# MoBA's attention scores in fp32r, from high and low parts of queries and keys with three products each, instead of fp32

## The reference, cut to what matters

```python
q_g, k_g, v_g, g_g, gk_lr, q_m, k_m, v_m = jnp.split(xn @ w_in, split_points, axis=-1)
scale = hd ** -0.5
s_own = (jnp.einsum('bhqd,bhsd->bhqs', qi, k_own, preferred_element_type=jnp.float32) * scale
         + bias_tab[:, rel_bucket(dist_own)])
s_own = jnp.where(dist_own >= 0, s_own, NEG)
probs = jax.nn.softmax(jnp.concatenate([s_past, s_own], axis=-1), axis=-1)
```

## Time and profile before

| | |
|---|---|
| median of 3 runs | 512.84 us (512.39 to 512.96) |
| the profiled execution | 512.54 us, span 510.4 us |
| mean granted TensorE clock | 0.997 |
| PE busy | 502.3 us (98%) |
| PEld busy | 410.9 us (81%) |
| DVE busy | 333.5 us (65%) |
| ACT busy | 278.4 us (55%) |
| POOL busy | 101.3 us (20%) |
| DMA | 119.18 MB, mean 234 GB/s |

### The profile page before, as it was taken

One profiled execution on the slowest core, in us unless ns is written; L12 is line 12 of the kernel. 1 busy time (PEld: TensorE's weight loads), 2 busy tenths in 40 slices (PEclk: granted clock), 3 DMA queues, 4 the chain that ended last, 5 costly groups with the idle time before them and its releaser, 6 DMA issues.

```text
span 510.4 us, 6961 instructions
## 1 busy us (share of the span) xinstructions
PE 502.3 (98%) x2472; PEld 410.9 (81%) x2472; DVE 333.5 (65%) x455; ACT 278.4 (55%) x361; POOL 101.3 (20%) x188
## 2 busy tenths in 40 slices
PE   8999999999999999999999999999999999999994
PEld 5888888888888888887787888888888888888883
DVE  4687556656566476788986875566565565474765
ACT  5784454443544456877675673544534543442747
POOL 1304232222220102220421010232222322110200
PEclk9999999999999999999999999999999999999998
DMA  7999888777778857749366976787777868639402
GB/s 256 377 307 369 268 251 254 210 235 236 221 239 313 274 183 255 296 136 345 112 227 200 315 249 186 239 265 216 229 243 252 241 227 231 223 133 280 158 7 82
DMA packets 78808, 119.18 MB, mean 234 GB/s; under 512 B 6110, under 2 KB 48520, under 8 KB 78656
## 3 DMA queue, kind: packets, MB, share of 16 engines
q1 hardware_dynamic: 69536, 93.07, 57.8%
q0 software_dynamic: 8944, 25.47, 14.5%
q10 hardware_dynamic: 304, 0.33, 0.2%
HBM read 107.04 MB, written 13.38 MB: 236 GB/s over the span
## 4 chain that ended last, share of the span: by engine, by line
PE 98%; ACT 0%; DVE 0%; issue 0%; DVEq 0%
PE acc L622 93%; PE side L622 2%; PE turn L622 2%; PE turn L662 1%; DVE h L1877 0%; DVE gate L1876 0%; ACT res L1378 0%; ACT w_hi L1292 0%; ACT hT_hi L1073 0%; ACT rtmp L1372 0%; DVE junk L1787 0%; ACT junk L1368 0%; PE side L662 0%; DVE rstd L1854 0%; DVE spare L1786 0%
## 5 line engine op out<-in xcount | busy, mean ns | idle before, releaser
L1405 DVE TENSOR_TENSOR w_lo<-raw,w_hi 128x2048 fp32r<-128x2048 f32 (+1 forms) x86 | 191.1, 2226 | 94.8 <-ACT w_hi L1049 94.7
L1049 ACT ACTIVATE w_hi<-raw 128x2048 fp32r<-128x2048 f32 (+1 forms) x86 | 160.2, 1867 | 103.8 <-PE acc L622 103.4
L622 PE MATMUL acc<-w_hi,hT_hi 128*128 128x512 f32 x496 | 194.5, 392 | 0.3 <-ACT w_hi L1292 0.3
L622 PE MATMUL acc<-w_hi,hT_lo 128*128 128x512 f32 x496 | 193.0, 390 | 0.0
L622 PE MATMUL acc<-w_lo,hT_hi 128*128 128x512 f32 x496 | 193.0, 389 | 0.0
L622 PEld LDWEIGHTS acc<-w_hi,hT_hi 128*128 128x128 f32 x496 | 93.0, 188 | 21.3 <-issue 1.2
L622 PEld LDWEIGHTS acc<-w_hi,hT_lo 128*128 128x128 f32 x496 | 93.1, 188 | 19.5
L622 PEld LDWEIGHTS acc<-w_lo,hT_hi 128*128 128x128 f32 x496 | 93.1, 188 | 19.0 <-DVE w_lo L1799 0.4
L531 POOL DMA_DIRECT2D act_in<-act_dram x92 | 50.1, 551 | 119.0 <-DMA act_dram<-act_sq 112.3
L622 PE MATMUL acc<-w_lo,a_hiT 128*128 128x512 f32 x176 | 68.5, 389 | 0.0
L622 PE MATMUL acc<-w_hi,a_hiT 128*128 128x512 f32 x176 | 68.5, 389 | 0.0
(11 more groups left out here) (207 smaller groups left out, 337.8 us busy)
## 6 DMA issues: line engine op xcount, KB each, us to landing
raw<-in_ffn_w_gu SPq DMA_DIRECT2D x82, 512.0 KB, 5.1
raw<-in_ffn_w_down SPq DMA_DIRECT2D x40, 512.0 KB, 5.2
raw<-in_w_in SPq DMA_DIRECT2D x24, 512.0 KB, 5.8
act_dram<-act_sq POOLq DMA_DIRECT2D x23, 256.0 KB, 5.5
act_in<-act_dram POOLq DMA_DIRECT2D x92, 64.0 KB, 3.6
raw<-in_w_out SPq DMA_DIRECT2D x8, 512.0 KB, 5.4
raw<-in_w_ple_gate SPq DMA_DIRECT2D x8, 512.0 KB, 5.5
raw<-in_ffn_w_gu SPq DMA_DIRECT2D x10, 256.0 KB, 5.8
```

The lines of the kernel that those rows point to most:

```text
L622: return nc.tensor.matmul(o, lhsT, rhs, start=start, stop=stop, skip_group_check=True)
L1049: A(hi, raw[:, slot, :nk * N], ACT.Copy).then_inc(hi_ready, 1)
L1405: V.tensor_tensor(lo, raw[:, slot, :nk * N], hi.bitcast(F32), ALU.subtract).then_inc(lo_ready, 1)
```

## The change

The scores are computed like the large matmuls: `q_mT` and `k_mT` become fp32r tiles that hold high parts, `q_lo` and `k_lo` are new and hold low parts, and each of the two matmuls of a head becomes three. DVE writes the low parts in three new steps `k_s0`, `k_s1` and `q_s`, and so is the last reader of the banks of `T_k0` and `T_k1`. The factor 1/8 moves from `T_q` to the evacuation of the queries, as a second scale `rstd_q` that DVE computes once. PE's step `sc0` moves from behind step 3 of unit 40 to behind step 0 of unit 41.

```diff
 MIX:
     (40, 1): ["T_k0", "T_k1"],
-    (40, 3): ["sc0.0", "sc0.1"],
+    (41, 0): ["sc0.0", "sc0.1"],
     (41, 1): ["sc1.0", "sc1.1"],
     (41, 2): ["lv1", "sc2.0", "sc2.1"],
...
-DVE_STEPS = [..., "Z0", "Z1", "lv0", "lo42",
-             "sc0", "lo43", "rc0", "sc1", "pr0", "sc2", "rc1", "Z2", "pr1", "rc2", "lv1", "Z3", "lv2", "lo44", ...
+DVE_STEPS = [..., "Z0", "Z1", "lv0", "k_s0", "k_s1", "q_s",
+             "lo42", "sc0", "lo43", "rc0", "sc1", "pr0", "sc2", "rc1", "Z2", "pr1", "rc2", "lv1", "Z3", "lv2", "lo44", ...
...
-            if s in ("T_r", "T_k0", "T_k1"):
+            if s == "T_r":
                 add(s, who="act")
...
+        rstd_q = sb("rstd_q", [P, M])
...
-        q_mT = at("q_mT", 46, [P, MH // 2, T])
+        q_mT = at("q_mT", 46, [P, MH // 2, T], F32R)
+        q_lo = at("q_lo", 68, [P, MH // 2, T], F32R)
-        k_mT = at("k_mT", 30, [P, MH // 2, T])
+        k_mT = at("k_mT", 30, [P, MH // 2, T], F32R)
+        k_lo = at("k_lo", 64, [P, MH // 2, T], F32R)
...
 PE, step sc:
-                    pe.wait_ge(turn_act, turned("T_k1"))
-                    pe.wait_ge(q_turned, 1)
+                    pe.wait_ge(turn_read, turned("T_k1"))
+                    pe.wait_ge(q_split, 1)
                     lo = 64 * (head % 2)
-                    q, k = q_mT[lo:lo + 64, head // 2, :], k_mT[lo:lo + 64, head // 2, :]
-                    mm(o[:, 0:P], q[:, 0:P], k[:, 0:P], True, True)
-                    mm(o[:, P:3 * P], q[:, P:T], k[:, :], True, True).then_inc(turn_done, 1)
+                    r = slice(lo, lo + 64)
+                    c = head // 2
+                    exact3(o[:, 0:P], q_mT[r, c, 0:P], q_lo[r, c, 0:P], k_mT[r, c, 0:P], k_lo[r, c, 0:P], True, True)
+                    exact3(o[:, P:3 * P], q_mT[r, c, P:T], q_lo[r, c, P:T], k_mT[r, c, :], k_lo[r, c, :], True, True
+                           ).then_inc(turn_done, 1)
...
 ACT:
-                A(k_mT[:, 2 * a:2 * a + 2, :].rearrange("p c t -> p (c t)"), turn[:, t % 2, :], ACT.Copy).then_inc(turn_act, 1)
+                A(k_mT[:, 2 * a:2 * a + 2, :].rearrange("p c t -> p (c t)"), turn[:, t % 2, :], ACT.Copy).then_inc(k_hi, 1)
...
+                if b == 1:
+                    act_e.wait_ge(rstd_q_set, 1)
...
-                      scale=rstd[:, 1, m:m + 1]).then_inc(acc_read, 1)
+                      scale=rstd_q[:, m:m + 1] if b == 1 else rstd[:, 1, m:m + 1]).then_inc(acc_read, 1)
...
-                      view(back[:], [[32, 8], [2 * P, 4], [1, 32]]), ACT.Copy, scale=MD ** -0.5).then_inc(q_turned, 1)
+                      view(back[:], [[32, 8], [2 * P, 4], [1, 32]]), ACT.Copy).then_inc(q_turned, 1)
...
 DVE:
+                elif s[:3] == "k_s":
+                    a = int(s[3])
+                    t = TURN[f"T_k{a}"]
+                    dve.wait_ge(k_hi, a + 1)
+                    dst, hi = [b[:, 2 * a:2 * a + 2, :].rearrange("p c t -> p (c t)") for b in (k_lo, k_mT)]
+                    V.tensor_tensor(dst, turn[:, t % 2, :], hi.bitcast(F32), ALU.subtract).then_inc(turn_read, 1)
+                elif s == "q_s":
+                    dve.wait_ge(q_turned, 1)
+                    ins = V.tensor_tensor(q_lo[:].rearrange("p k (m i e) -> p (k m) i e", m=M, i=4),
+                                          view(back[:], [[32, 8], [2 * P, 4], [1, 32]]),
+                                          q_mT[:].rearrange("p k (m i e) -> p (k m) i e", m=M, i=4).bitcast(F32), ALU.subtract)
+                    ins.then_inc(q_split, 1)
...
             rms(1)
+            V.tensor_scalar(rstd_q[:], rstd[:, 1, :], MD ** -0.5, None, ALU.mult).then_inc(rstd_q_set, 1)
             for s in DVE_STEPS:
                 step(s)
```

More of the change, by code:

```diff
@@ L92 @@
              "hi47", "sc3", "nm3", "pv0", "nat4", "pv1", "hi48", "nat5", "pvg", "pv2", "groot", "pv3", "hi49"]
-DVE_STEPS = ["h11", "lo38", "lo39", "lr", "g_sq", "z", "dot", "lo40", "zmin", "la", "q_sq", "lo41", "Z0", "Z1", "lv0", "lo42",
-             "sc0", "lo43", "rc0", "sc1", "pr0", "sc2", "rc1", "Z2", "pr1", "rc2", "lv1", "Z3", "lv2", "lo44", "pr2", "sc3",
+DVE_STEPS = ["h11", "lo38", "lo39", "lr", "g_sq", "z", "dot", "lo40", "zmin", "la", "q_sq", "lo41", "Z0", "Z1", "lv0", "k_s0", "k_s1", "q_s",
+             "lo42", "sc0", "lo43", "rc0", "sc1", "pr0", "sc2", "rc1", "Z2", "pr1", "rc2", "lv1", "Z3", "lv2", "lo44", "pr2", "sc3",
              "lv3", "rc3", "lo45", "pr3", "pv0", "lo46", "lo47", "pv1", "lo48", "pvg", "gg", "pv2", "o_g", "pv3", "lo49"]
@@ L363, in build @@
         q_turned = sem("q_turned")
+        rstd_q_set = sem("rstd_q_set")
+        q_split = sem("q_split")
+        k_hi = sem("k_hi")
         lg_ready = sem("lg_ready")
```

## The result

The changed kernel takes 514.02 us, the median of 13 runs (513.69 to 514.32), against 512.81 us for the kernel before in the same session. The ratio is 1.0026, with a 95% interval of 1.0019 to 1.0033: slower, by about 1.2 us. The forecast was 513.3 us and "no change that can be told"; the measured time is inside the range, but close to the 514.2 us of the short-call rival, not to the likeliest case, and the 1.2 us are more than the 1.03 that the prediction took as the least that can be told.

A forecast was written before the change was run, and what follows sets the result against it. PE was taken to bound the kernel, running without waits. A hold at sc2 (+0.38) and 0.05 more for sc2 and sc3 gave +0.43 on 512.54, 512.97; with 0.30 to the median, 513.3 us, range 512.4 to 514.6.

The forecast's parts named there:

- short-call rival: At the scores on PE: a 128-column fp32r matmul costs four passes, 0.213 us; +1.35 us, 514.2 us; chance 0.20.
- the likeliest case: Whole kernel: PE's extra weight loads plus a wait for DVE at sc2, +0.43 us, 513.3 us; chance 0.60.
- That PE never waits, so its stream counts one for one: PE, first stage to last: it runs without waiting, so anything added to its stream arrives at the end in full.
- So fp32 is four passes, and the heads overlap: Scores on PE before the change: four passes over 384 columns, 0.64 us, two heads side by side in 0.86 us.
- the heads in turn: Rival at the scores on PE: the two heads no longer overlap, 0.68 us a pair, 2.7 in all, 515.6 us; chance 0.10.
- 0.68 us a head, +0.025 a pair, from 0.109 and 0.118: Scores on PE: three 128-column matmuls at 0.109 and three 256-column at 0.118, against 0.655 us in fp32.
- 2.36 us on DVE and the late bank at sc2: DVE's three splits delay release of sc1's second bank to 238.46, so PE waits 0.33 us at sc2.
- the loads' 0.10: Scores on PE: weight loads eat the saved pass, adding 0.025 us a pair, 0.10 us in four.
- Three passes instead of four as a gain: Rival at the scores on PE: loads hide, a pair loses 0.16 us; 512.9 us, or 512.2 without stall; chance 0.10.

## Why the prediction came out as it did

- **That PE never waits, so its stream counts one for one:** held. 1.2 us more in the pieces of the pairs, 1.2 us in the median.
- **"So fp32 is four passes, and the heads overlap":** right for the kernel before. The step that failed is the next one, that the heads of the changed kernel would overlap in the same way. The rival had it the other way round and all or nothing: the heads in turn, 2.7 us. It was in between: three records of head 0, instead of one, are started before head 1 may begin, 0.28 us a pair, 1.1 us in four. The profile before bore the clue. I used "the four fp32 records of a head stood ahead too, and the heads ran side by side" as evidence that six would not matter; it was evidence for four only.
- **0.68 us a head, +0.025 a pair, from 0.109 and 0.118:** held. With the heads together a pair is 0.89 us, and 0.43 with one product. The saved pass does go to the loads.
- **2.36 us on DVE and the late bank at sc2:** the work measured 2.34. The wait is real, shown alone at 0.23 us; in the changed kernel PE, slowed by its own pairs, came 0.43 us after the bank was free. The forecast of +0.43 was 0.33 of wait and the loads' 0.10; what happened is +1.2 from the pairs and nothing from DVE. The two do not add, because either delay covers the other, the relation that the prediction used for the short-call rival.
- **Three passes instead of four as a gain:** the records show no gain. With the order mended, the time is 0.4 us above the kernel before by median and not clearly different.
- **The chances:** slower by over 0.2% had 0.28. The sum for the likeliest case missed a term of 1.1 us, larger than everything in it. That the range held is luck: it reached up to 514.6 for the short call, whose 0.31 us a pair happened to be the size of the lag and the loads together (0.28 + 0.03). The short call itself did not occur.

## What to carry to other kernels

Small matmuls on different row halves overlapped fully here only where the program brought them close together: write them in turn, product by product with the heads alternating, when one half has more than four records (five were not tried). Count records, not calls: an fp32 call is two. Before splitting fp32 into three products, compare weight loads with passes: a single pass of 128 columns costs its load, and over the 128 and 256 columns of a head three products (0.68 us) are no cheaper than four passes (0.655), while the splits are new work elsewhere. And a kernel with every engine in a fixed order has many ties of a few tenths of a microsecond: moving lo43 to remove a wait of 0.24 us made one of 1.3.

## What the runs showed of the hardware that was not expected

The first record of the other row half started when three records of this half were still unstarted: after record 1 of 4 (0.014 us later in fp32, 0.013 in fp32r), 3 of 6 in fp32r (0.006), 3 of 6 in fp32 (0.006) and 9 of 12 in fp32 (0.006). The runs show this only for two halves of 64 rows and a program in which one half's records all come first, with semaphore waits between the halves; what in PE sets the three was not settled. The Trainium skill ("TensorE: Matmul & The Clock Gate", Part 3) says that matmuls start strictly in program order; for two row halves these records differ, and they decide. Also, going from 128-row to 64-row matmuls and back costs 0.20 us a time here (2.95 for 2.75 us in the earlier trace rows) whether the scores are fp32 or fp32r: six projection matmuls behind a pair take 1.59 us in the kernel before and in the changed one.
